# Columns spread over the partitions by transposes, gates in two passes, and the last block's order of work

## The reference

```
# odd mixer: 8 gate columns per token, beside q, k, v and the output gate
ig = soft_cap(ig_pre + gb[0]);  lf = log_sigmoid(soft_cap(fg_pre + gb[1]))
# hybrid layer, delta-rule branch, 4 heads of width 128, chunks of 64 tokens
qkv = silu(causal_depthwise_conv(qkv, conv_w))        # 4 taps
beta = sigmoid(beta_logit);  g = -exp(a_log) * softplus(a_logit + dt_bias)
q, k = l2_normalize(q), l2_normalize(k)
g = cumsum(g) per chunk;  decay = exp(g_i - g_j), causal
a = strict((k*beta) @ k.T * decay);  t_inv = inverse(1 + a)
u = t_inv @ (v*beta);  w = t_inv @ (k*beta*exp(g));  qk = q @ k.T * decay
```

## Time and profile before

| | us |
|---|---|
| median of 3 runs (959.72 to 962.24) | 961.87 |
| the profiled execution's own time | 959.94 |
| its span | 958.2 |
| TensorE busy | 918.0 (96%) |
| VectorE busy | 635.2 (66%) |
| ScalarE busy | 482.9 (50%) |
| GpSimd busy | 34.2 (4%) |

### The profile page before, as it was taken

How to read it: one execution, slowest core, us unless ns; L and a number is a source line. 1 busy time by engine, 2 the same in 40 slices (tenths; PEclk the granted TensorE clock), 3 DMA queues, 4 the chain that set the end, 5 groups by cost and what they waited for, 6 DMA issues and landing times.

```text
span 958.2 us, 14654 instructions
## 1 busy us (share of the span) xinstructions
PE 918.0 (96%) x6312; PEld 818.2 (85%) x6312; DVE 635.2 (66%) x786; ACT 482.9 (50%) x630; POOL 34.2 (4%) x25
## 2 busy tenths in 40 slices
PE   5999999999999999999999999999797999989997
PEld 5989888899999998988789999998696998877775
DVE  4798656577676766784769766666767574446563
ACT  7675456473343435655666333444555653347441
POOL 0000000000000000000000000000000164000000
PEclk9999999999999999899999999999788999999999
DMA  9544434456666654353456666664333233424331
GB/s 373 178 171 151 157 132 163 167 192 247 233 240 235 243 189 157 132 176 132 143 183 228 236 236 227 220 235 161 109 133 132 88 133 133 133 71 158 107 127 44
DMA packets 23728, 165.49 MB, mean 173 GB/s; under 512 B 2640, under 2 KB 2896, under 8 KB 4336
## 3 DMA queue, kind: packets, MB, share of 16 engines
q1 hardware_dynamic: 22176, 159.39, 47.3%
q0 software_dynamic: 1056, 4.34, 1.2%
q10 hardware_dynamic: 432, 0.82, 0.2%
HBM read 163.49 MB, written 1.05 MB: 172 GB/s over the span
## 4 chain that ended last, share of the span: by engine, by line
PE 88%; DVE 6%; ACT 4%; issue 1%; DMA 0%; DVEq 0%; ACTq 0%
PE lin L511 15%; PE lin L512 15%; PE lin L513 15%; PE acc L511 11%; PE acc L512 11%; PE acc L513 11%; PE acc L690 1%; DVE w_lo L1599 1%; PE acc L749 1%; ACT w_hi L1163 1%; PE lin L626 1%; PE lin L863 1%; ACT arena L1546 1%; PE lin L596 1%; PE lin L609 1%
## 5 line engine op out<-in xcount | busy, mean ns | idle before, releaser
L1599 DVE TENSOR_TENSOR w_lo<-raw,w_hi 128x2048 fp32r<-128x2048 f32 x138 | 318.4, 2315 | 153.7 <-ACT w_hi L1163 152.5
L1163 ACT CAST w_hi<-raw 128x2048 fp32r<-128x2048 f32 x138 | 262.2, 1906 | 178.5 <-DMA raw<-in_weights 108.3
L511 PE MATMUL lin<-h_hi,w_hi 128*128 128x256 f32 x736 | 212.4, 289 | 7.3 <-ACT arena L1345 5.3
L512 PE MATMUL lin<-h_lo,w_hi 128*128 128x256 f32 x736 | 210.3, 286 | 0.0
L513 PE MATMUL lin<-h_hi,w_lo 128*128 128x256 f32 x736 | 210.1, 286 | 0.0
L511 PEld LDWEIGHTS lin<-h_hi,w_hi 128*128 128x128 f32 x736 | 143.3, 195 | 8.8 <-ACT arena L1345 5.7
L512 PEld LDWEIGHTS lin<-h_lo,w_hi 128*128 128x128 f32 x736 | 143.3, 195 | 0.3
L513 PEld LDWEIGHTS lin<-h_hi,w_lo 128*128 128x128 f32 x736 | 143.2, 195 | 0.0
L511 PE MATMUL acc<-w_hi,f_hi 128*128 128x512 f32 x288 | 112.5, 391 | 0.0
L512 PE MATMUL acc<-w_lo,f_hi 128*128 128x512 f32 x288 | 112.3, 390 | 0.0
L513 PE MATMUL acc<-w_hi,f_lo 128*128 128x512 f32 x288 | 112.2, 390 | 0.0
(11 more groups left out here) (333 smaller groups left out, 1109.8 us busy)
## 6 DMA issues: line engine op xcount, KB each, us to landing
raw<-in_weights SPq DMA_DIRECT2D x150, 1024.0 KB, 4.9
rowbuf<-in_rows POOLq DMA_DIRECT2D x6, 512.0 KB, 4.2
x<-in_x_in SPq DMA_DIRECT2D x2, 512.0 KB, 4.5
arena<-in_const_even POOLq DMA_DIRECT2D x1, 1024.0 KB, 10.0
out<-x SPq DMA_DIRECT2D x2, 512.0 KB, 2.6
cst<-in_const ACTq DMA_DIRECT2D x1, 576.0 KB, 9.3
colbuf<-in_cols ACTq DMA_DIRECT2D x1, 159.0 KB, 5.9
msk<-in_masks POOLq DMA_DIRECT2D x1, 144.0 KB, 5.7
```

Source lines behind the costliest of these rows:

```text
L511: pe.matmul(dst, st_hi, mv_hi, start=first, stop=False)
L512: pe.matmul(dst, st_hi, mv_lo, start=False, stop=False)
L1163: act.copy(w_hi[:, o % SPLIT, :], raw[:, j % RAW, :]).then_inc(hi_done, 1)
L1599: dve.tensor_tensor(w_lo[:, j % RAW, :], r, hi.bitcast(F32), ALU.subtract).then_inc(tile_split, 1)
```

## The change

- A column of `stat` (a value per token) is spread as a row over all partitions by one transpose whose input is the column repeated 128 times (`column_as_row`). It replaces the product of ones with a diagonal in `broadcast_r` and `inverse_lengths`, and the one-hot products of rows for `dbeta`, `drow` and `deg`. The diagonals on VectorE and the turned beta row with its copy go.
- The high and low part of the gate weights lie side by side, and one product of the high part of h has both as its moving operand (16 columns). A second product (low part of h, 8 columns) follows. VectorE adds the two parts (`add_gate_parts`).
- The inverse lengths are written to `acc`, not to a `lin` pair.
- In the last block the orders change: ScalarE does the cast, the row exponentials and `dz`'s copy ahead of q's SiLU; VectorE splits `dv`'s second tile ahead of the convolution of q; TensorE makes the columns, `drow` and q's squares ahead of `dv`'s second half, and `dkt` ahead of the scores. GpSimd adds each tap when it is there.

```diff
@@ -139,7 +139,7 @@
     g += ["n1a0", "n1a1", "*mq", "mk", "mv0", "mv1", "*mrow", "mo0", "*mden", "mo1", "*y1a", "*y1b"]
     g += mlp(1)
-    g += ["n2a0", "n2a1", "*dk", "dq", "dz", "*dkn", "dv", "*dqn", "*dbeta", "*drow", "*dkt", "bq",
+    g += ["n2a0", "n2a1", "*dk", "dq", "dz", "dv", "*drow", "*dbeta", "*dkt", "bq",
           "*deg", "*dvt", "bk", "bv", "bz", "gd0", "*gate", "gd1", "*dyt", "*bt0", "*bt1", "*bt2",
           "gm0", "*by", "gm1", "*byt", "*y2a", "*y2b"]
...
@@ -264,7 +264,8 @@
-        wg_hi, wg_lo = (h[:, 8, 0:64].rearrange("p (k m) -> p k m", k=DC) for h in (h_hi, h_lo))
+        wg = h_hi[:, 8, 0:128].rearrange("p (k a m) -> p k a m", k=DC, a=2)
+        wg_hi, wg_lo = wg[:, :, 0, :], wg[:, :, 1, :]
         def col(name, i=0, n=1, rows_=P):
...
@@ -468,8 +469,8 @@
                 if i == 5:
-                    pool.wait_ge(taps_ready, 1)
                     for o in range(1, 4):
+                        pool.wait_ge(taps_ready, 1 + o)
                         at = S_AT["pre"] + (o - 1) * 1024
                         v, tap = (arena[:, a:a + 1024].rearrange("p (b t) -> p b t", b=4) for a in (S_AT["v"], at))
...
@@ -657,10 +658,14 @@
                 products(1, 1, range(8)).then_inc(tile_used, 1)
+            def column_as_row(out, j):
+                return pe.transpose(out, stat[:, j:j + 1].to_broadcast([P, P]), ident)
+
             def broadcast_r():
-                after(rd_ready)
-                pe.matmul(acc[:, 1024:1024 + T], ones, arena[:, LEAD["diag"]:LEAD["diag"] + T],
-                          start=True, stop=True).then_inc(rb_done, 1)
+                after(r_done, 2)
+                for t in range(TT):
+                    mm = column_as_row(acc[:, 1024 + t * P:1024 + (t + 1) * P], 10 + t)
+                mm.then_inc(rb_done, 1)
             def lead_turned(name):
...
@@ -820,10 +825,11 @@
                 after(wg_ready)
                 for t in range(TT):
-                    at = GATE_ACC["z"] + 8 * t
+                    at = GATE_ACC["z"] + 16 * t
                     for k in range(DC):
-                        h = [part[:, k, t * P:(t + 1) * P] for part in (h_hi, h_lo)]
-                        mm = passes(acc[:, at:at + 8], *h, wg_hi[:, k, :], wg_lo[:, k, :], k == 0, k == DC - 1)
+                        hi, lo = (part[:, k, t * P:(t + 1) * P] for part in (h_hi, h_lo))
+                        pe.matmul(acc[:, at:at + 16], hi, wg[:, k, :, :], start=k == 0, stop=False)
+                        mm = pe.matmul(acc[:, at:at + 8], lo, wg_hi[:, k, :], start=False, stop=k == DC - 1)
                 mm.then_inc(gates_done, 1)
...
@@ -847,11 +853,11 @@
                 return mm
-            def to_columns(which, base):
+            def to_columns(which, base, first=0):
                 for i, w in enumerate(which):
                     for t in range(TT):
-                        at = (i * TT + t) * H
+                        at = first + (i * TT + t) * H
                         mm = pe.transpose(acc[:, at:at + H], row(w, base)[:, t * P:(t + 1) * P], ident[0:H, 0:H])
                 mm.then_inc(cols_done, 1)
...
@@ -936,12 +942,26 @@
                 mm.then_inc(cols_done, 1)
-            def inverse_lengths(name):
-
+            def inverse_lengths():
+
+                after(length_ready)
+                for i in range(8):
+                    mm = column_as_row(acc[:, 1024 + i * P:1024 + (i + 1) * P], i)
+                mm.then_inc(norm_done, 1)
+
+            def head_transposes(name, src):
                 open_pair(name)
-                after(diag_ready)
-                for i in range(8):
-                    mm = pe.matmul(pair(name)[:, i * P:(i + 1) * P], ones, at("dia", P, i * P), start=True, stop=True)
+                for t in range(TT):
+                    for h in range(H):
+                        i = t * H + h
+                        mm = pe.transpose(pair(name)[:, i * P:(i + 1) * P], at(src, P, h * T + t * P), ident)
+                mm.then_inc(lin_special, 1)
+
+            def columns_as_rows(name, columns):
+
+                open_pair(name)
+                for i, j in enumerate(columns):
+                    mm = column_as_row(pair(name)[:, i * P:(i + 1) * P], j)
                 mm.then_inc(lin_special, 1)
...
@@ -951,40 +971,33 @@
             sum_squares("sqk")
             after(sp_ready)
-            turned_columns(GATE_ACC["brow"], stat[:, 128:136])
             turned_columns(GATE_ACC["row"], gate("sum")).then_inc(crow_done, 1)
             fill("dz", 0)
-            inverse_lengths("dkn")
+            after(rows_ready)
+            inverse_lengths()
             fill("dz", 1)
             fill("dv", 0)
+            after(erow_ready)
+            to_columns((7, 8, 4, 3), S_AT["rows"], 512)
             after(cols_read)
             sum_squares("sqq")
+            after(cols_read)
+            columns_as_rows("drow", [96 + t * H + h for h in range(H) for t in range(TT)])
             fill("dv", 1)
-            inverse_lengths("dqn")
-            after(erow_ready)
+            after(l2_done)
+            inverse_lengths()
+            columns_as_rows("dbeta", [128 + t * H + h for h in range(H) for t in range(TT)])
+            head_transposes("dkt", "k")
             after(cols_read)
-            to_columns((7, 8, 4, 3), S_AT["rows"])
-            to_all_partitions("dbeta", 0, base=S_AT["rows"])
-            to_all_partitions("drow", 7, base=S_AT["rows"])
-            after(cols_read)
-            after(l2_done, 2)
+            after(l2_done)
             for i in range(8):
                 k = at("k", P, i * P)
             mm.then_inc(sc_done, 1)
-            def head_transposes(name, src):
-                open_pair(name)
-                for t in range(TT):
-                    for h in range(H):
-                        i = t * H + h
-                        mm = pe.transpose(pair(name)[:, i * P:(i + 1) * P], at(src, P, h * T + t * P), ident)
-                mm.then_inc(lin_special, 1)
-
-            head_transposes("dkt", "k")
             fill("bq", 0)
-            to_all_partitions("deg", 3, P, P, base=S_AT["rows"])
+            columns_as_rows("deg", [124 + h for h in range(H)])
             fill("bq", 1)
             after(silu_ready, 3)
...
@@ -1483,26 +1496,30 @@
             copy_out("dq", at("pre", 1024, 1024))
             root_lengths()
-            after(crow_done, 2)
-            act.copy(srow(0), acc[0:H, GATE_ACC["brow"]:GATE_ACC["brow"] + T])
             split_until(LAST["dq"] + 4)
+            ahead("dz")
+            act.wait_ge(rows_ready, 1)
+            act.activation(srow(3), srow(9), ACT.Exp)
+            act.activation(srow(4), srow(2), ACT.Exp).then_inc(erow_ready, 1)
+            copy_out("dz", at("z"), ACT.Silu)
             conv_silu(S_AT["q"])
             act.wait_ge(silu_ready, 4)
             act.activation(at("sqq"), at("q"), ACT.Square).then_inc(l2_sq, 1)
-            copy_out("dz", at("z"), ACT.Silu)
-            act.wait_ge(rows_ready, 1)
-            act.activation(srow(3), srow(9), ACT.Exp)
-            act.activation(srow(4), srow(2), ACT.Exp).then_inc(erow_ready, 1)
             root_lengths()
             split_until(LAST["dz"] + 4)
             copy_out("dv", at("pre", 1024, 2048))
-            filled(act, "dbeta")
-            act.copy(at("beta"), pair("dbeta")[:, :]).then_inc(freed("dbeta"), 1)
-            for o in (0, 1, 2, 3):
+            read_out(act, "dv")
+
+            def taps(o):
                 for b in range(4):
                     d = at("v", T, b * T) if o == 0 else at("pre", T, (o - 1) * 1024 + b * T)
                     ins = act.activation(d, at("pre", T, 2048 + b * T), ACT.Copy, scale=col("convd", (8 + b) * 4 + 3 - o))
-            ins.then_inc(taps_ready, 1)
+                ins.then_inc(taps_ready, 1)
+            taps(0)
+            filled(act, "dbeta")
+            act.copy(at("beta"), pair("dbeta")[:, :]).then_inc(freed("dbeta"), 1)
+            for o in range(1, 4):
+                taps(o)
             after(w_diff_ready)
             act.activation(at("D"), at("D"), ACT.Exp).then_inc(w_exp_ready, 1)
...
@@ -1685,12 +1702,7 @@
                     dve.reciprocal(r, stat[:, 34 + t:35 + t]).then_inc(r_done, 1)
                     after(r_done)
-                    if bias is None:
-                        at = LEAD["diag"] + t * P
-                        ins = dve.tensor_scalar(arena[:, at:at + P], ident, r, None, ALU.mult)
-                        if t == 1:
-                            ins.then_inc(rd_ready, 1)
-                    else:
+                    if bias is not None:
                         at = LEAD["xs"] + t * D
                         dve.tensor_scalar(arena[:, at:at + D], x[:, t, :], r, None, ALU.mult).then_inc(xn_ready, 1)
...
@@ -2024,6 +2036,12 @@
                 link(dve.scalar_tensor_tensor(sp, sp, 2.0, q2, ALU.mult, ALU.add))
+            def add_gate_parts():
```

(47 more changed lines are left out.)

10 lines of the change are left out of this document (5 added, 5 removed).

## The result

Before: 962.06 us, median of 4 runs (959.72 to 963.42). After: 939.56 us, median of 4 runs (937.90 to 941.56). The ratio is 0.977, 95% interval 0.9741 to 0.9798: 22.5 us less. The forecast was 942.0, with a range of 936 to 948.

What follows compares the result with a forecast made beforehand. TensorE, busy 96% of the span, was taken as the bound. Savings 0.45 + 2.3 + 2.4 + 12.85 + 0.65 = 18.65 off 959.94 gave 941.3, plus 0.9 for middling runs: 942; own range 939.5 to 944.5, with rivals 936 to 948.

Steps and rivals of the forecast that it cites:

- What bounds the kernel: Whole kernel: TensorE, busy 96% of the span; only less TensorE time or fewer and shorter holes shorten it.
- Prices: TensorE: gate product 0.11 us with 8 or 16 columns; repeated-column transpose 0.106, upper bound 0.21, adding 3.6 for 34.
- The gates at `mq`: Gates to gate sums at `mq`: 2.3 us saved (bounds 1.8 and 2.7), TensorE then waiting for VectorE's log1p, ending at 404.0.
- The gates at `dk`: Gates at `dk` to the end of `dq`: 2.4 us saved, between 1.55 with unchanged half clock and 4.95 at full clock.
- E to `bq`: Last block, from the end of `dq` (E) to `bq`: 46.55 us becomes 33.7, a saving of 12.85, summed by terms.
- The hole's cause: Hole of 5.40 us before `dv`: TensorE is held by the order on ScalarE and VectorE, not by late data.
- Does the other side keep up?: Last block: ScalarE and VectorE deliver in time, with margins of 2.0, 1.7 and 2.4 us; Y ready at E+51.6.
- the first rival: A wait in the hole's place: one of the 2 us margins overrun by 3 to 6 us, 945 to 948; chance 0.14.
- Half clock gone at both gates: Half clock disappears from the gate stages at `mq` and `dk`: 938 to 939, at best 936; chance 0.12.
- Transposes that do not hold the clock: Transposes act as idle time: one half-clock stretch gives 944 (chance 0.04); slower than the kernel before, chance 0.02.
- the worst case: All from E to Y (54 us) at half clock: costs 27 to 54 us, giving 950 to 977 and more.
- Nothing from the reordering: `drow` opens `dz`'s pair; its copy late by the full 5.4 again: only some 13 saved, 947 to 948; chance 0.02.

Runs made afterwards that it cites:

- after_again: The kernel after, unaltered, timed a second time: 942.31 us beside 962.01 for the kernel before, ratio 0.9794.
- gates_only: Kernel before with only the gates in two passes and VectorE's two small additions: 956.71 us, ratio 0.9943.
- spreads: Kernel before with repeated-column transposes in place of diagonals and 4-partition products, order of work and PSUM pairs otherwise nearly as before: 957.81 us, ratio 0.9959.
- dz_early_only: Kernel before with only ScalarE's copy of `dz` moved ahead of q's convolution: 956.20 us, ratio 0.994.
- pairs_only: Kernel before with only the two inverse lengths written to the accumulator instead of PSUM pairs: 956.10 us, ratio 0.9935.
- after_act_order: Kernel after with ScalarE's row exponentials and `dz` copy back behind q's convolution: 948.71 us, ratio 0.9863 to the kernel before.
- after_more_turns: Kernel after with q's inverse lengths and `dbeta` turned four times over, 48 transposes more: 945.02 us, ratio 0.9825 to the kernel before.
- better3: better2 with the first token tile's gate products run between the lead's products of the first and second tiles: 932.70 us, ratio 0.9696 to the kernel before.
- better2: better with VectorE's part of the gate sums at `mq` also put ahead of two splits: 940.15 us, ratio 0.9761 to the kernel before.
- better: Kernel after with log1p ahead of q's convolution at `mq`, and `bk`'s first half ahead of `dvt`: 939.12 us, ratio 0.9765 to the kernel before.
- gates3: Kernel after with three gate products again for 14 of 16 blocks (46 instead of 32): 948.15 us, ratio 0.9856 to the kernel before.

## Why the forecast was right, step by step

*What bounds the kernel.* Right: all of the gain is TensorE's, 19.1 in busy time and about 3 in holes. The prediction also counted 34 of the new transposes; there are 42 (22 into the accumulator and 20 into pairs). At the measured pace that changes nothing, but its upper bound for slow ones would have been 4.5 and not 3.6.

*Prices.* The gate products at 0.11 with 8 or 16 columns: right, no cost for the wider ones (3.55 for 32). Repeated columns at the pace of ordinary transposes: right, 0.106; the upper bound of 0.21 is excluded.

*The gates at `mq`.* 2.75 against 2.3. Right in the mechanism, TensorE waits for VectorE's log1p. That came at 402.9 and not at 404.0: the whole stage began 0.6 earlier, and VectorE waited 0.3 for ScalarE's tanh where it had waited 1.3.

*The gates at `dk`.* The mis-sized term: 4.95 in the profiled execution against 2.4, and 1.75 to 1.85 in the five profiles whose half clock there lasts 6.8 us (after_again and gates_only among them). What I called a rival is the state of single executions: among seven profiles with 32 products in a row, half clock after the gates at `dk` lasted 6.8 us in five, 3.4 in one and 0 in one. 2.4 lies between what single executions show, and none of the seven has it. It stands for a mean of such cases, and that is partly why the sum lands between the two medians.

*E to `bq`.* 12.8 against 12.85, and 33.75 or 33.8 in all six profiles in which the new order there stands as it is. The hole, `dv`'s clock, 0.85 for the inverse lengths, the single-pass rows, the scores at full clock and the wait of 0.4 for `dv`'s copy are all there. But the terms are not separate. Taken alone, spreads save 4.1 there instead of 6, since what they save ahead of the hole is lost in it, `dv` behind it loses 0.7, and a wait of 0.8 comes. Of the two cures of the hole alone, one left the half clock at the scores at 3.4 us and the other had 6.8. My attribution of the scores' half clock to the 4-partition products holds as far as the runs go: in gates_only, dz_early_only and pairs_only these products stay and half clock comes at the scores; in the nine profiles without them it never does. The 8 products of this kind at `mrow`, in the odd mixer, stand in every profile, and half clock begins within 1.3 us of their end in six of thirteen. So 8 of them were followed by it at times and 16 in a row each time, but the rule behind it is not shown.

*The hole's cause.* I had put it down to the order on ScalarE and VectorE. That is one of two sufficient cures. The other is that the inverse lengths no longer take a pair, which pairs_only shows alone; the prediction did not name it.

*Does the other side keep up?* The last step of Y on VectorE, to be set beside the earlier trace rows:

```profile
758.35 2.07 DVE L2234 TENSOR_TENSOR arena<-cst,arena 128x1024 f32<-128x1024 f32 x1
```

Y is ready at 760.4, E+51.2 (51.6 forecast), and TensorE turns it at 763.05, E+53.8 (54.0): margin 2.6. No margin was overrun, so the first rival did not come, but after_act_order shows how near it is: exponentials that are late by the length of q's convolution cost 6.4, a little over what that rival had said (3 to 6).

*The rivals.* Half clock gone at both gates: in no profile of the kernel after, but gone at `dk` in the profiled execution (937.9, inside its 936 to 939); no median lies there. Transposes that do not hold the clock: refuted by after_more_turns. Its price for the worst case was wrong: 27 to 54 us on top of 942 give 969 to 996, where the prediction, which took the saving off twice, has 950 to 977. Nothing from the reordering: refuted.

Open: why half clock comes after the same 32 products in one execution and not in another, and why, in two halves, they drew none. better3 also changes when the gates come and how much idle time stands ahead at `dk`: in three profiles (before, pairs_only, better2) 3.4 us of half clock came within 1.1 us of the wait of 2.2 there, which better3 does not have. At `mq` no idle time changed, but there the profile of better had no half clock after 32 products in a row either. So the trace of better3 doesn't tell these apart.

## What to carry to other kernels

A hole that ends in a copy can be closed from either side, by an earlier copy or by work that no longer needs the buffer; try each alone, and then see what the first now feeds in the new order. Parts of a change timed alone do not add up where a hole or a half-clock stretch takes back what one of them gives, so cost them together along one path. Where an engine waits for another in front of a stage, move small independent products of the next stage into the wait, and then read from the rows what they hid and what the clock gave: here 1.5 us were hidden, and most of the 7.45 came with a higher clock, whose cause stays open.

## What the runs showed of the hardware that was not expected

- Weights read as one column repeated 128 times load at full pace: 0.106 to 0.109 per fp32 transpose, as for ordinary blocks.
- 7.8 us of fp32 transposes in a row kept the full clock, and the products behind them had it too.
- The half clock comes in stretches of 3.4, 6.8 and three times 10.2 us (a last one, at the end of each trace, aside), at the same few places: from within or behind the gate products, after a hole, and after products on 4 partitions. In all thirteen profiles one of 3.4 or 6.8 us comes near 675, around a wait of 3.6 us for `h_lo` at the start of `dk`. After 46 or 48 gate products in a row it was 6.8 or 10.2 us in the profiles of before, gates3, pairs, spreads and dz_early; after 32 in a row anything from 0 to 6.8; after 16 and 16 apart, none.
- Runs of one kernel with a lower mean clock are the longer ones, but the clock does not set all of the difference. The six runs of after_again range from 937.80 at a mean clock of 0.993 to 943.74 at 0.988, and the five at 0.988 still range from 940.32 to 943.74.
